# A modulation product in plain fp32 on four column groups of TensorE instead of in split fp32r

## The reference, cut to what matters

```
c_act  = silu(c)[:, None, :]                  # one vector of 1024
cc_act = silu(c_ctx)[None, None, :]           # a second one
for i in range(2):
    mx = split(c_act  @ ada_w[i] + ada_b[i], 6)   # ada_w[i]: 1024 x 6144, fp32
    mc = split(cc_act @ ada_w[i] + ada_b[i], 6)
    h_x = rms_norm(x, norm1_g[i]) * (1 + mx[1]) + mx[0]
    ...                                       # attention (i = 0), retention (i = 1), SwiGLU
    x = x + mx[2] * out_x
```

## Time and profile before

| What | Value |
|---|---|
| Median of three executions | 2799.11 us |
| Span of the profiled execution, first to last instruction | 2793.3 us |
| TensorE busy | 2667.5 us, 95% |
| VectorE busy | 1506.9 us, 54% |
| ScalarE busy | 1300.6 us, 47% |
| Mean granted TensorE clock | 0.979 of full speed |
| Read from memory | 395.72 MB, 142 GB/s over the span |

### The profile page before, as it was taken

How to read it: one execution, slowest core, us unless ns; L and a number is a source line. 1 busy time by engine, 2 the same in 40 slices (tenths; PEclk the granted TensorE clock), 3 DMA queues, 4 the chain that set the end, 5 groups by cost and what they waited for, 6 DMA issues and landing times.

```text
span 2793.3 us, 49776 instructions
## 1 busy us (share of the span) xinstructions
PE 2667.5 (95%) x18388; PEld 2388.5 (86%) x18388; DVE 1506.9 (54%) x2322; ACT 1300.6 (47%) x1928; POOL 100.7 (4%) x87
## 2 busy tenths in 40 slices
PE   5999999999998998999999999999989999999998
PEld 3846657888887996999899999789989999978998
DVE  4467865333226325555555565765545656566554
ACT  4357763222224333444445458644444545854443
POOL 3000000000000000000000002100000000210000
PEclk9989999999999999999999999999999999999999
DMA  7235551332323332365565555346646555544563
GB/s 247 68 121 175 180 157 60 108 98 90 98 91 106 97 123 67 122 193 175 157 182 166 166 174 166 106 136 181 180 140 193 157 174 170 158 125 144 162 181 117
DMA packets 398685, 398.67 MB, mean 143 GB/s; under 512 B 17361, under 2 KB 396769, under 8 KB 398545
## 3 DMA queue, kind: packets, MB, share of 16 engines
q1 hardware_dynamic: 395680, 390.25, 46.1%
q0 software_dynamic: 2864, 6.57, 0.7%
HBM read 395.72 MB, written 1.05 MB: 142 GB/s over the span
## 4 chain that ended last, share of the span: by engine, by line
PE 80%; issue 9%; DVE 4%; ACT 3%; DMA 1%; POOL 1%; SPq 0%; ACTq 0%; DVEq 0%; POOLq 0%
PE acc L708 61%; PE acc L695 5%; PE acc L759 3%; PE wk L818 2%; PE wk L778 1%; ACT w_hi L1061 1%; DMA raw<-in_ada_w_dram 1%; DVE w_lo L1543 1%; PE acc L841 1%; PE wk L841 1%; PE acc L731 1%; PE wk L768 1%; POOL XC L643 1%; PE acc L944 1%; PE wk L944 1%
## 5 line engine op out<-in xcount | busy, mean ns | idle before, releaser
L1543 DVE TENSOR_TENSOR w_lo<-raw,w_hi 128x1024 fp32r<-128x1024 f32 x752 | 926.2, 1239 | 858.2 <-ACT w_hi L1061 845.7
L708 PE MATMUL acc<-h_hi,w_hi 128*128 128x256 f32 (+1 forms) x3696 | 1119.1, 303 | 48.0 <-DVE h_lo L1645 22.3
L708 PE MATMUL acc<-h_lo,w_hi 128*128 128x256 f32 (+1 forms) x3696 | 1111.6, 301 | 0.0
L708 PE MATMUL acc<-h_hi,w_lo 128*128 128x256 f32 (+1 forms) x3696 | 1111.3, 301 | 0.0
L1061 ACT CAST w_hi<-raw 128x1024 fp32r<-128x1024 f32 x752 | 771.6, 1033 | 555.9 <-PE acc L708 472.7
L708 PEld LDWEIGHTS acc<-h_hi,w_hi 128*128 128x128 f32 x3696 | 716.7, 194 | 75.6 <-DVE h_lo L1645 25.5
L708 PEld LDWEIGHTS acc<-h_lo,w_hi 128*128 128x128 f32 x3696 | 717.9, 194 | 20.8
L708 PEld LDWEIGHTS acc<-h_hi,w_lo 128*128 128x128 f32 x3696 | 717.0, 194 | 20.9
L708 PE MATMUL acc<-hid_hi,w_hi 128*128 128x256 f32 (+1 forms) x1056 | 319.8, 303 | 0.0
L708 PE MATMUL acc<-hid_hi,w_lo 128*128 128x256 f32 (+1 forms) x1056 | 318.3, 301 | 0.0
L708 PE MATMUL acc<-hid_lo,w_hi 128*128 128x256 f32 (+1 forms) x1056 | 317.4, 301 | 0.0
(11 more groups left out here) (330 smaller groups left out, 2479.1 us busy)
## 6 DMA issues: line engine op xcount, KB each, us to landing
raw<-in_w_in_dram SPq DMA_DIRECT2D x100, 512.0 KB, 4.0
raw<-in_ada_w_dram SPq DMA_DIRECT2D x96, 512.0 KB, 3.8
raw<-in_ffn_w_in_dram SPq DMA_DIRECT2D x88, 512.0 KB, 3.5
raw<-in_ffn_w_gate_dram SPq DMA_DIRECT2D x88, 512.0 KB, 4.5
raw<-in_ffn_w_up_dram SPq DMA_DIRECT2D x88, 512.0 KB, 4.0
raw<-in_ffn_w_down_dram SPq DMA_DIRECT2D x80, 512.0 KB, 3.9
raw<-in_ret_w_qkvg_dram SPq DMA_DIRECT2D x48, 512.0 KB, 3.6
raw<-in_ffn_w_out_dram SPq DMA_DIRECT2D x40, 512.0 KB, 3.5
```

The lines of the kernel that those rows point to most:

```text
L708: mm = pe.matmul(o, ws[:, s, k, c], xs[:, kk, t], start=(u == 0 and k == 0 and i == 0), stop=(last and k == nk - 1 and i == 2))
L1543: dve.tensor_tensor(w_lo[:, s, 0:nk, :], raw[:, s, 0:nk, :], w_hi[:, s, 0:nk, :], ALU.subtract).then_inc(lo_done, 1)
```

## The change

- `modulation_unit` waits for the DMA of its unit instead of for the split, and multiplies `raw` itself, in plain fp32. The stationary operand is `c_wide`, 128 x 32 for each k-chunk: the two vectors in columns 0 and 1 and zeros in the other 30. Chunk k goes to columns 32k to 32k+31 of the array and to partitions 32k to 32k+31 of the block (`tile_position=(0, 32 * k)`). A unit is 4 matmuls instead of 8.
- ScalarE and VectorE no longer split these 96 units. The counters `hi_done` and `lo_done` no longer count them (`split0`, `Job.split`).
- A slot of `raw` that holds such a unit is free when TensorE has used it, so SyncE waits for `units_used` ahead of its next DMA. Four such units can be in flight or waiting, where there were eight before.
- A block is now 128 x 256 with a partial sum for each chunk. `ada_s` has 128 partitions, the copies have the same 256 elements on each, and `turn_chunk` multiplies 128 x 128 with a 128 x 2 `sel` that picks partitions 0 and 1 of each group and adds the four.
- `c_wide` lies in `nomask`. VectorE clears that again after the first attention (`c_zero`), and the later attentions wait for it.

```diff
-            ("ada_skip", ...), ("ada_s", [4, 6 * D], F32))
+            ("ada_skip", ...), ("ada_s", [P, 6 * D], F32))
...
-        "sel": np.repeat(np.eye(2), 2, axis=0)[np.minimum(p, 3)] * (p < 4)[:, None],
+        "sel": np.stack([p % 32 == w for w in range(2)], axis=1),
...
-        c_parts = sb("c_parts", [P, DC, 4], F32R)
+        c_wide = nomask[:].rearrange("p (k m) -> p k m", m=32)
...                                                     # SyncE, stream
-                        sp.wait_ge(lo_done, job.unit(l, it, p) + 1)
+                        held = after if p < SLOTS else name
+                        if held in ADA:
+                            sp.wait_ge(units_used, job.unit(l, it, p) + 1)
+                        elif held and name in ADA:
+                            sp.wait_ge(lo_done, J[held].split(l, J[held].iters - 1, J[held].body - SLOTS + p) + SLOTS + 1)
+                        elif held:
+                            sp.wait_ge(lo_done, job.split(l, it, p) + 1)
...                                                     # TensorE, modulation_unit
-                unit_ready(job, None, it, p)
+                pe.wait_ge(load[p % SLOTS], job.loaded(None, it, p))
                 for k in range(KCH):
-                    for i, ws in enumerate((w_hi, w_lo)):
-                        mm = pe.matmul(acc[0:4, b % 2, 0, 0:S], c_parts[:, u * KCH + k, :], ws[:, p % SLOTS, k, :],
-                                       start=(u == 0 and k == 0 and i == 0), stop=(u == 1 and k == KCH - 1 and i == 1))
+                    mm = pe.matmul(acc[32 * k:32 * k + 32, b % 2, 0, 0:S], c_wide[:, u * KCH + k, :], raw[:, p % SLOTS, k, :],
+                                   start=(u == 0), stop=(u == 1), tile_position=(0, 32 * k), skip_group_check=True)
                 mm.then_inc(units_used, 1)
...                                                     # turn_chunk
-                return pe.matmul(dst, ada_s[0:4, c * P:(c + 1) * P], sel[0:4, :], start=True, stop=True)
+                return pe.matmul(dst, ada_s[:, c * P:(c + 1) * P], sel[:, :], start=True, stop=True)
...                                                     # ScalarE and VectorE, beside_first: the splits go
-                for k in range(SIDE_UNITS):
-                    if side_step(k) == i:
-                        name, it, p = side_unit(k)
-                        split(J[name], None, it, p)
...                                                     # VectorE, start of the kernel
-            head("ada0a")
-            rest("ada0a", ada, None, [lambda: None, inputs])
-            head("q0", None, "ada0a", ada)
+            ada(0)
+            ada(1)
+            inputs()
+            for it in range(2, J["ada0a"].iters):
+                ada(it)
+            head("q0")
```

More of the change, by code:

```diff
@@ L111, in unit, with split @@
         return self.unit0 + p + it * self.body + (l * self.unit_step if self.unit_step else 0)
+    def split(self, l, it, p):
+        return self.unit(l, it, p) - self.unit0 + self.split0
     def block(self, l, it, b):
@@ L168, with unsplit_before, job_before @@
 JOBS = plan()
+ADA = ("ada0a", "ada0b", "ada1")
+def unsplit_before(name):
+    return sum(J.iters * J.body for n, J in JOBS.items() if n in ADA and J.unit0 < JOBS[name].unit0)
+for name in JOBS:
+    JOBS[name].split0 = JOBS[name].unit0 - unsplit_before(name)
+def job_before(name):
+    order = FIRST + SECOND
+    return order[order.index(name) - 1] if name != order[0] else None
 NORMS1 = 7
@@ L495, in one @@
                         sp.dma_start(dst, s).then_inc(load[p % SLOTS], 16)
+                before = job_before(name)
                 if job.iters == 1:
                     one(0)
+                elif before is None or (before in ADA) != (name in ADA):
+                    one(0, before)
+                    with sp.Fori(1, job.iters) as it:
+                        one(it)
                 else:
@@ L662, in unit_ready @@
             def unit_ready(job, l, it, p):
-                pe.wait_ge(lo_done, job.unit(l, it, p) + SLOTS + 1)
+                pe.wait_ge(lo_done, job.split(l, it, p) + SLOTS + 1)
             def slot_free(job, l, it, b):
@@ L860, in _ @@
             turn_parameters(wk[:, 3], range(1))
[L861 removed]
+            pe.wait_ge(c_wide_ok, 1)
             for it in range(2):
@@ L1541, in split @@
                 s, nk = p % SLOTS, job.unit_chunks[p]
-                dve.wait_ge(hi_done, job.unit(l, it, p) + 1)
+                dve.wait_ge(hi_done, job.split(l, it, p) + 1)
                 dve.tensor_tensor(w_lo[:, s, 0:nk, :], raw[:, s, 0:nk, :], w_hi[:, s, 0:nk, :], ALU.subtract).then_inc(lo_done, 1)
@@ L1701, in attention, with ada @@
                         beside(i)
[L1703 to L1712, removed]
+            def ada(it):
+                for b in range(J["ada0a"].per):
+                    block_done(J["ada0a"], None, it, b)
+                    at = (it * J["ada0a"].per + b) * COLS
+                    dve.tensor_copy(ada_s[:, at:at + COLS], acc[:, b, 0, 0:S]).then_inc(acc_free, 1)
             def square_last(name, l=None):
@@ L1888, in _ @@
                     dve.tensor_tensor(qk[:, n, 0:S], rot_b[:, b % 2, 0, :], rot_b[:, b % 2, 1, :], ALU.add).then_inc(hqk, 1)
-                beside_first(c - 11)
-            attention("first", groups_first(), None, beside_first)
+            attention("first", groups_first(), None)
             head("wo0")
             dve.wait_ge(pt_ok, ITEMS0)
+            dve.wait_ge(units_used, J["ada1"].unit(None, J["ada1"].iters - 1, J["ada1"].body - 1) + SLOTS + 1)
+            dve.memset(nomask[:], 0.0).then_inc(c_zero, 1)
             modulations(2, 0, mod[:, 0, 16:48, :], 16, 48)
```

24 lines of the change are left out of this document (10 added, 14 removed).

## The result

The changed kernel takes 2763.8 us (median of 4 runs, 2761.5 to 2771.4) against 2799.0 us before on the same chip: ratio 0.988, with an interval of 0.986 to 0.989, or 35 us less. The forecast was 2811 us, in a range of 2790 to 2882 us. What came is near the rival that all four groups run side by side (2754 us).

The account below looks back on a forecast made before the run. It took TensorE to bound attention and a slot's round trip to bound the first 16 units. Terms 14 + 6 + 1 - 4 - 5 = +12 us gave span 2805.3, plus 5.8, 2811 us; range 2790 to 2882 us.

Parts of the forecast that it names:

- the rival that all four groups run side by side: Modulation units' four column groups overlap wholly, 0.44 us a unit; -45 us in all, 2754 us; chance 0.16.
- The unit in a stream: Modulation unit on TensorE, 80 units: 1.11 us instead of 0.93 us by program-order starts, +14 us.
- Changes of shape: TensorE around units: 0.12 us gap at the exit in 72 steps, less 3 us at turns; +6 us, bounds 0 and +12.
- Half clock: Five units from 165 to 184 us, at 1.2 GHz, pay their extra 0.18 us twice: +1 us.
- the staircase: Modulation units: starts keep program order, each second record follows its first, 5 periods, 1.11 us a unit; 2811 us, chance 0.50.
- Waits that go: TensorE's 1.78 us wait ahead of the first scores and 2.5 us behind ScalarE's copies go: -4 us, bounds 0 and -4.
- hidden splits: Splits on VectorE and ScalarE beside attention are hidden behind TensorE; taking them away gives nothing by itself there.
- The start: First 16 units, bound by a slot's round trip, go from landing to product without splits: -5 us, bounds 0 and -8.
- Transfers: SyncE's landings for units in attention stay hidden though it now waits for products; uncovered, up to 4 us a late unit.
- a sign of being wrong: A TensorE wait for `raw` in attention would make the prediction wrong in a way not priced.
- The serial rival: Column groups don't overlap, a unit takes 1.78 us; +72 us in all, 2871 us; chance 0.28.

Follow-up runs that it names:

- two_blocked: Changed kernel with chunks 0 and 1 on column group 0, chunks 2 and 3 on group 1; 2786.5 us, 0.996 of the kernel before.
- experiment 8: Also called warm_gap: changed kernel with ten unused plain fp32 matmuls filling TensorE's wait ahead of the rotation loop; 2771.1 us, 0.990 of the kernel before.
- experiment 3: Same run as two_blocked: changed kernel with chunks 0, 1, 2, 3 on column groups 0, 0, 1, 1; 2786.5 us, 0.996 of the kernel before.
- the pairs: Changed kernel with the 80 units beside attention laid two to a step, 40 steps instead of 72; 2753.4 us, 0.984 of the kernel before.
- dummy_splits: Changed kernel with the split work of the 80 side units put back on ScalarE and VectorE, unused; 2763.5 us, 0.987 of the kernel before.

## Why the prediction was wrong

**The unit in a stream: this step failed.** "If starts keep the order of the program, chunk 1's first record can start with chunk 0's second, and so on: 5 periods" gave 1.11 us and +14 us. Its condition doesn't hold (two_blocked), and the unit is 2 periods and 0.14 us. Counted from start to start over attention at full clock (experiment 8), the 71 units there take 39.5 us where they took 66.3 us: 27 us less, where the term had 13 us more. The period of 0.222 us was right (0.216 to 0.24), and so was the bound for all four side by side, 0.44 us. What failed was the weighing of the order of issue against the independence of the groups, and the text itself said that no row decides it; the sum and half of the chance were put on the order all the same. Nothing in the trace of before spoke for it: no two of its matmuls in a row lay on different column groups.

The rule of the Trainium skill, "TensorE: Matmul & The Clock Gate", "Part 3: Packing small matmuls", which was drawn on for this, is half right here: column groups overlap (3.2 times for four, where it has 2.38 times for three), with starts a few ns apart (6.5 ns; it has 4). That starts keep the order of the program the traces contradict (experiment 3), and also its sentence that a load overlaps a matmul in flight only where the row groups differ: all four chunks use all rows, and the eight loads took 0.16 us beside the first bunch. The measurement decides. The kernel before had shown the second point: its loads of 0.084 us fitted between matmuls of 256 columns on all rows that started only 0.116 us apart.

**Changes of shape.** Forecast 0.12 us at the exit, 72 times, less 3 us at the turns: +6. Measured: 0.57 us less the 0.43 us of two periods (of 0.216 us) is 0.14 us a visit, and the first transposition behind it takes 0.056 us more than before, 14 us in 72 visits. The turns, with the transposition ahead of them, take 4.5 us less in attention. That is +9 or +10: the mechanism was right and the term some 3 us short. The 0.14 us is also what the pairs get back. One reading was off: L818's second record starts at 252.78 us and not 252.73, for the 0.43 us used was the mean over its records, and the last one takes 0.38 us. The gap ahead of L759 is 0.09 us, and it is the same before and after the change, since the unit starts 0.306 us behind the last record of the scores in both.

**Attention as a whole.** From start to start, at full clock (warm_gap) against before: units 26.8 us less, turns and the transpositions ahead of them 4.5 us less, first transpositions behind units 3.5 us more, and scores 1.5 us more, which is the wait for `raw` behind them. That is 26.3 us, the difference of the windows.

**Half clock.** Forecast +1 in the staircase, from units alone. It is most of what the profiled execution lacks to the rival's -45 us (its span is 21 us above that rival's 2748 us). At half clock a stretch loses half its length: 17 us in attention cost 8.5 us in the profiled execution (190.9 - 8.5 = 182.4 us, against 183.1 us at full clock), 1.7 us in the later one (184.8 - 1.7 = 183.1 us). At the start it cost 4.9 us. In the rotation loop the rival had -8 us (wait and units); measured is +0.7 and +0.1 us, with 14 and 10 us more at half clock than in the first profile before, which cost 7 and 5 us. That the clock did this is shown; that the change caused it is not, since nothing that was tried moved it for sure.

**Waits that go.** Forecast -4 us. Neither went whole: 0.7 us is left ahead of the scores where 1.78 us stood, and the weight loads still wait 1.6 us for copies, in 2 places, where it was 2.5 us in 5. That hidden splits were worth nothing was right (dummy_splits).

**The start.** -5 us forecast, -3.0 and -1.2 us measured against the first profile before, and -7.8 and -6.1 us against the second. In the first pair TensorE's last unit ends 8 us sooner, as the removed casts and subtractions promised; the rest went to the clock.

**Transfers.** Forecast hidden. TensorE waits 1.4 us for `raw` in all of attention, which the prediction had named as a sign of being wrong and not priced; it is small. Behind attention the changed kernel's profiles are 1.9 to 3.3 us shorter than the two of the kernel before, for which there was no term; where that comes from stays open.

**The serial rival** was priced +72 us. With all chunks on one group it came to +59 us. In its profile attention takes 67 us more than before, near what the rival's units had there, and the stretch from q0 to the scores nothing more, where the rival had some 12 us of units and half clock. That loop had 13.7 us of half clock, as little as any profile here. That kernel isn't quite the rival either, since its turns have 32 rows.

## What to carry to other kernels

In this kernel small matmuls on different column groups of the array ran side by side, in each order of writing that was tried. To price such a unit, count the records of the longest group, times one period, and add 0.14 us a visit. Put visits together as far as the landed data allow. When no row tells between two mechanisms and the answer turns the sign, put the chance between them and not on a story about order. When a forecast comes true, check its parts as well: the pairs gained the 10 us expected of them, and only about half of it by the mechanism expected. A helper engine at 79% beside a TensorE that never waits can lose all of that work for nothing.

## What the runs showed of the hardware

- A plain fp32 matmul is two records, and four of them on four column groups over all 128 rows take 2 periods (0.24 us from bunch to bunch), on two groups 4, on one 8 (0.216 us each).
- Records on different groups start 6.5 ns apart (13 ns in two_blocked), and not in the order of the source.
- A visit of 128 x 32 tiles costs 0.14 us beyond its periods, however many units it has (0.57 us for one, 1.00 us for two). The first 128 x 128 transposition behind it takes 0.165 us instead of 0.109 us, and takes as long straight behind the 64 x 128 scores.
- The granted clock stayed at 1.2 GHz for 13.7 to 41 us in the rotation loop, in warm_gap with TensorE busy for 31.7 of 32 us, and differently from one execution to the next.
